# Reordered norm start and attention pair boundaries, and 64 moving columns in small matrix products of a hybrid diffusion backbone

## The chip, the cores and the metric

The kernel runs on one core of one Trainium2 chip. The metric is the device time of one execution in microseconds; of several executions the median is given. Everything below is on that single core: TensorE (PE in the profile, with its weight loads as PEld), VectorE (DVE), ScalarE (ACT), GpSimd (POOL) and SyncE (SP), which here only issues DMAs.

## The reference

A backbone of two layers over 512 latent and 256 context tokens of width 1024. Each layer normalises the tokens, shifts and scales them by vectors made from a condition, mixes them, and then runs a gated convolutional feed-forward network. Layer 0 mixes by retention with 4 heads, layer 1 by neighbourhood attention with 16 heads of width 64. Cut to what matters here:

```
for i in range(2):
    sh1, sc1, g1, sh2, sc2, g2 = split(silu(c) @ ada_w[i] + ada_b[i], 6)      # latent tokens
    csh1, csc1, ...            = split(silu(c_ctx) @ ada_w[i] + ada_b[i], 6)  # context tokens
    h  = rmsnorm(x, norm1_w[i]) * (1 + sc1) + sh1
    hc = rmsnorm(ctx, norm1_w[i]) * (1 + csc1) + csh1
    y, yc = retention(h, hc) if i == 0 else neighbourhood_attention(h, hc)
    x = x + g1 * y;  h2 = rmsnorm(x, norm2_w[i]) * (1 + sc2) + sh2;  x = x + g2 * conv_ffn(h2)
    # the same for ctx in layer 0
return rmsnorm(x, final_norm_w)
```

## The kernel before, in words

Activations lie with features on the 128 partitions: `x` is 8 blocks (k = 0 to 7) of 128 features by 768 tokens. Each large matrix is split into a high part and a rest (`w_hi`, `w_lo`, and `h_hi`, `h_lo`), and each product is three matrix products: high by high, high by rest, rest by high. `split()` on ACT makes `w_hi` from a raw 512 KB chunk (L873), `split()` on DVE makes `w_lo` (L1298), and `next_chunk()` on PE waits for it. SP streams the chunks through two slots. Each engine's order is written out by hand; semaphores join them.

**The start.** ACT squares the 8 blocks of `x`, DVE adds them, PE sums over partitions (`token_sums`, L448, with a moving operand `ones` of two columns), ACT takes roots (L903), DVE their reciprocals (`one_over`, L1329), and PE spreads them over the partitions (`spread_roots`, L455). ACT copies the spread row into `ss` (L930). Meanwhile SP has issued, in this order, `small`, `x`, the condition rows, and then for each k one 1 MB block `ada_start[k]`, with a raw weight chunk behind block 0 and block 2.

In `start_norm` DVE then goes through k = 0 to 7. `scale(k)` makes the scale vector by two multiply-and-reduce instructions over 1024 elements (L1340, L1342) and one small one (L1348). `shift(k)` takes the shift vector: for k in `PE_SHIFTS` = (1, 2, 4, 6, 7) PE makes it in `shift_row(k)` (L440: 8 matrix products, each recorded as two fp32 passes, with two moving columns) and DVE only adds a bias (L1357); for k = 0, 3, 5 DVE makes it with two more reductions and L1362. `rooted_x(k)` multiplies by the spread root (L1365), ACT applies scale and shift (L939) and rounds (`h_hi`, L943), and `low(k-1)` makes `h_lo` (L1369). For k = 2, 4, 6 a `split()` follows.

PE multiplies the normalised tokens with the first head's value weights (`token_values`, L538): for each k it waits for `h_lo` of that k and runs 18 products of 512 columns. `shift_row(4)`, `(6)` and `(7)` stand between them, and behind k = 4 also `idle(9)`, nine 128-column products whose result nobody reads (L465). Such fillers also stand ahead of it, in `start()`. After `token_values` PE runs the key and query projections (L403).

**The attention pairs.** In layer 1 two heads form a pair, c = 0 to 7. In `pair` PE runs `block_scores(i)` for 8 blocks (L689), `turn_probs(i)` (transposes of the probabilities, L697), the projections of the next pair in parts of a few products (`part`, L724: values, keys, queries), and `pair_values(0)`, `pair_values(1)` (L710). At a pair's end `turn_pair_values` transposes the next pair's values (L772). The next pair starts with `acc_taken[1]` and `q_taken`, then two block scores, then half of a value projection, then block score 2 and `turn_probs(0)`. `q_taken` counts once per pair, after both heads' queries have been split into `nq_hi` (four ACT instructions, L1193) and `nq_lo` (two DVE instructions, L1796).

After the queries ACT and DVE have a tail before the next pair's first maximum: a weight `split()`, `take_half(c, 1)` (L1209) and `add_halves(1)` (L1813), which finish the head output `both`; `take_turned_values` (L1201, L1806), which stores the transposed values and frees the accumulator that `turn_probs(0)` needs; and the split of `both` into `no_hi` and `no_lo` (L1235, L1846). Only then come `maximum(0)` (L1763), `exps(0)` (L1164), and `scale_probs(0)` (L1769, L1770), which `turn_probs(0)` waits for.

Of the kernel before, what the change touches and what calls it, by code (L numbers as in the profile page):

```python
# [37 lines left out]
P = 128  # L38
# [23 lines left out]
PE_SHIFTS = (1, 2, 4, 6, 7)  # L62
# [74 lines left out]
def backbone(nc, x_in, weights, ada_first, ada, cond_rows, small_in, bias_in, masks_in, park, out):  # L137
    ctx = ExitStack()
    with ctx:
# [88 lines left out]
        sums = o_ps[:, 3, 0:2 * TT]  # L228
        spread = o_ps[:, 0:2, :].rearrange("p a t -> p (a t)")
        shifts = [o_ps[:, n % 2, 2 * n:2 * n + 2] for n in range(len(PE_SHIFTS))]  # L230
# [136 lines left out]
        def _(pe):  # L367
# [43 lines left out]
            def start():  # L411

                pe.wait_ge(set_up, 1)
                idle(16, ones[:, :])
                pe.wait_ge(const_in, 16)
                for k in range(2, KC):
                    pe.wait_ge(sq_added, k)
                    idle(3)
                token_sums(KC, TOK)
                idle(4)  # L420
                pe.wait_ge(root_done, 1)
                idle(4)
                spread_roots(PARTS)
                idle(5)
                pe.wait_ge(cond_done, 1)
                shift_row(1)
                idle(4)
                shift_row(2)
                idle(12)

            def shift_row(k):

                n = PE_SHIFTS.index(k)
                pe.wait_ge(ada_start_in[k], 16)
                if n == 0:
                    pe.wait_ge(spread_copied, 1)
                elif n > 1:
                    pe.wait_ge(shift_taken, n - 1)
                for j in range(KC):
                    mm = nc.tensor.matmul(shifts[n], ada_start[k][:, 1, j * P:(j + 1) * P], silu_c[:, j, :],  # L440
                                          start=(j == 0), stop=(j == KC - 1))
                mm.then_inc(shift_made, 1)

            def token_sums(n, width):

                pe.wait_ge(sq_added, squares_added.up(n))
                for t in range(width // P):
                    mm = nc.tensor.matmul(sums[:, 2 * t:2 * t + 2], ss[:, t * P:(t + 1) * P], ones[:, 0:2], start=True, stop=True)  # L448
                mm.then_inc(sums_done, 1)
# [23 lines left out]
            def final_sums(width, ends=False):  # L473

                if not ends:
                    pe.wait_ge(lo_split, chunk.now() + 1)
                half = LAT if width == TOK else LAT // 2
                pe.wait_ge(sq_added, squares_added.up(KC) - 1)
                for t in range(width // P):
                    mm = nc.tensor.matmul(sums[:, 2 * t:2 * t + 2], ss[:, t * P:(t + 1) * P], ones[:, 0:2],  # L480
                                          start=(t == 0), stop=False)
                mm.then_inc(sq_added, 1)
                keep_busy(4)
                pe.wait_ge(sq_half, halves.up())
                for t in range(width // P):
                    if t == half // P:
                        pe.wait_ge(sq_done, squares_added.now())
                    mm = nc.tensor.matmul(sums[:, 2 * t:2 * t + 2], S[1][:, t * P:(t + 1) * P], ones[:, 0:2],
                                          start=False, stop=(t == width // P - 1))
                mm.then_inc(sums_done, 1)  # L490
# [32 lines left out]
            def token_values(first, ready):  # L523
# [3 lines left out]
                if first:  # L527
                    open_at(1)
                for s in range(4):
                    wh, wl = next_chunk()  # L530
                    for d in range(2):
                        k, last = 2 * s + d, s == 3 and d == 1
                        if ready is not None:
                            ready(k)
# [7 lines left out]
                        if first and k == 4:  # L542
                            idle(9, None, o_ps[:, 0, P:2 * P])
                            shift_row(PE_SHIFTS[4])
                    if s < 3:
                        mm.then_inc(v_used, 1)
                    if first and s < 2:
                        shift_row(PE_SHIFTS[2 + s])

# [183 lines left out]
            def queries():  # L733
                if q_left.began():
                    pe.wait_ge(q_taken, q_left.now())
                q_left.up()
# [38 lines left out]
            def pair(following):  # L775

                pe.wait_ge(acc_taken[1], A.taken[1].now())
                pe.wait_ge(q_taken, q_left.now())
# [7 lines left out]
                for i in range(8):  # L786
                    if i + 2 < 8:
                        block_scores(i + 2)
# [67 lines left out]
        def _(act):  # L856
# [41 lines left out]
            def root(n, width, loaded=False):  # L898
# [4 lines left out]
                nc.scalar.activation(rms[:, 0:t], sums[:, 0:2 * t].rearrange("p (t c) -> p t c", c=2)[:, :, 0],  # L903
# [306 lines left out]

            def pair(c, following):
# [32 lines left out]
            take_turned_values()  # L1244
# [31 lines left out]
        def _(dve):  # L1276
# [57 lines left out]
            def start_norm():  # L1334
# [3 lines left out]
                def row(k, r, made):  # L1338
# [6 lines left out]
                def scale(k):  # L1345
                    dve.wait_ge(ada_start_in[k], 16)
                    row(k, 0, k)
# [5 lines left out]
                def shift(k):  # L1353
                    if k in PE_SHIFTS:
                        n = PE_SHIFTS.index(k)
                        dve.wait_ge(shift_made, n + 1)
                        nc.vector.tensor_scalar(own_shift(k), shifts[n], ada_b[:, 0, k:k + 1], None, ALU.add)\  # L1357
# [8 lines left out]

                def low(k):
# [424 lines left out]
            def take_queries():  # L1792
# [5 lines left out]
                ins.then_inc(q_taken, 1)  # L1798
# [15 lines left out]

            def pair(c, following):
                dve.wait_ge(bias_done, biases_made.up(6))
                maximum(0)
                maximum(1)
                scale_probs(0)
                for i in range(8):  # L1820
# [4 lines left out]
                    probs_lo(i)  # L1825
                    if i == 5:
                        add_halves(0)
# [13 lines left out]
                add_halves(1)  # L1841
                if following:
                    take_turned_values()
# [14 lines left out]
            take_turned_values()  # L1858
# [191 lines left out]
```

## Time and profile before

| | |
|---|---|
| median of 3 executions | 2020.12 us (2018.02 to 2022.12) |
| the profiled execution, its own time | 2016.33 us |
| its span in the trace | 2014.4 us |
| PE busy | 1975.9 us, 98% of the span |
| DVE busy | 1293.6 us, 64% |
| ACT busy | 717.7 us, 36% |
| mean granted clock of PE | 0.994 of full speed |

The span is the stretch that the trace covers; 1.9 us of the execution lie around it. Busy time is that in which an engine has an instruction under way. The granted clock is the share of full speed (2.4 GHz) that PE was given: it is either 1.0 or 0.5 (1.2 GHz). The chain of waits is followed back from the last instruction, at each step to whatever released it.

### The profile page before, as it was taken

The numbers are of one execution on the slowest core, as the hardware profiler recorded it, in microseconds if no ns is written. First come the engines' busy times: TensorE is split into PE (matmuls) and PEld (weight loads), VectorE is DVE, ScalarE is ACT, GpSimd is POOL, SyncE is SP. The second block draws the span as 40 slices with busy tenths as digits, with TensorE's granted clock in tenths as the row PEclk, the third lists the DMA queues.
The fourth block names the chain that finished last, engine by engine and source line by source line (L and its number), as shares of the span: only waits on it lengthen the run. The fifth ranks groups of instructions, "written<-read, shape, count | busy, mean of one in ns | idle before, by whom it ended". The sixth has DMA issues, their size and how long they took to land.

```text
span 2014.4 us, 29078 instructions
## 1 busy us (share of the span) xinstructions
PE 1975.9 (98%) x10648; PEld 1692.1 (84%) x10648; DVE 1293.6 (64%) x1984; ACT 717.7 (36%) x1111; POOL 93.2 (5%) x161
## 2 busy tenths in 40 slices
PE   8999999999999999999999999999999999999998
PEld 7888888888888888888888888888888778788886
DVE  7866635744745677766664567766777677467376
ACT  5423223223313343312331233455555543234143
POOL 0000000000000000000000000111111000000000
PEclk8999999999999999999999999999999999999999
DMA  7231311221222112233224324421111322223223
GB/s 300 84 95 63 113 61 59 95 73 63 85 94 63 53 62 95 94 125 115 94 94 129 112 94 127 143 68 48 50 50 48 103 75 95 94 95 103 93 94 105
DMA packets 51268, 186.56 MB, mean 93 GB/s; under 512 B 5680, under 2 KB 5680, under 8 KB 51184
## 3 DMA queue, kind: packets, MB, share of 16 engines
q1 hardware_dynamic: 37744, 136.73, 20.6%
q0 software_dynamic: 13440, 48.63, 7.5%
q8 instruction: 62, 1.02, 0.2%
q14 instruction: 22, 0.18, 0.0%
HBM read 181.15 MB, written 4.19 MB: 92 GB/s over the span
## 4 chain that ended last, share of the span: by engine, by line
PE 90%; DVE 5%; ACT 2%; issue 1%; DMA 1%; SPq 0%; DVEq 0%; ACTq 0%; POOLq 0%
PE acc L403 60%; PE acc L724 5%; PE acc L664 4%; PE o_ps L538 4%; PE o_ps L574 3%; PE o_ps L724 2%; PE acc L538 2%; PE acc L561 2%; PE acc L503 2%; PE acc L759 2%; PE acc L697 1%; PE o_ps L689 1%; PE o_ps L710 1%; ACT nq_hi L1193 1%; DVE w_lo L1298 1%
## 5 line engine op out<-in xcount | busy, mean ns | idle before, releaser
L873 ACT ACTIVATE w_hi<-raw 128x1024 fp32r<-128x1024 f32 x223 | 235.7, 1057 | 582.7 <-PE acc L403 467.2
L1298 DVE TENSOR_TENSOR w_lo<-raw,w_hi 128x1024 fp32r<-128x1024 f32 x223 | 272.8, 1223 | 256.9 <-ACT w_hi L873 255.1
L403 PE MATMUL acc<-h_hi,w_hi 128*128 128x512 f32 x1520 | 434.4, 349 | 3.4 <-ACT u L1074 1.8
L403 PE MATMUL acc<-h_hi,w_lo 128*128 128x512 f32 x1520 | 434.8, 349 | 0.0
L403 PE MATMUL acc<-h_lo,w_hi 128*128 128x512 f32 x1520 | 434.7, 349 | 0.0
L403 PEld LDWEIGHTS acc<-h_hi,w_hi 128*128 128x128 f32 x1520 | 244.3, 188 | 43.9 <-ACT u L1074 2.5
L403 PEld LDWEIGHTS acc<-h_hi,w_lo 128*128 128x128 f32 x1520 | 244.4, 188 | 39.0
L403 PEld LDWEIGHTS acc<-h_lo,w_hi 128*128 128x128 f32 x1520 | 243.6, 188 | 38.4
L1467 DVE SCALAR_TENSOR_TENSOR x<-acc,mod,x 128x512 f32<-128x512 f32 (+3 forms) x137 | 82.0, 633 | 152.0 <-PE acc L403 121.8
L403 PE MATMUL acc<-act_hi,w_hi 128*128 128x512 f32 (+1 forms) x396 | 120.1, 357 | 2.0 <-DVE x L1467 2.0
L403 PE MATMUL acc<-act_hi,w_lo 128*128 128x512 f32 (+1 forms) x396 | 120.0, 357 | 0.0
L403 PE MATMUL acc<-act_lo,w_hi 128*128 128x512 f32 (+1 forms) x396 | 119.4, 355 | 0.0
L1409 DVE CUSTOM_DVE_ANT_0 ada_raw<-ada_raw,silu_rows 128x1024 f32<-128x1024 f32 x80 | 97.8, 1222 | 7.5 <-DMA ada_raw<-in_ada_dram 5.7
L320 POOL DMA_DIRECT2D ada_raw<-in_ada_dram x79 | 41.9, 530 | 1167.0 <-DVE mod_new L1409 1167.0
L1085 ACT ACTIVATE act_hi<-scratch 128x768 f32 (+3 forms) x44 | 32.6, 740 | 142.5 <-DVE scratch L1668 142.5
L1659 DVE SCALAR_TENSOR_TENSOR scratch<-u,taps,scratch 128x769 f32<-128x769 f32 (+1 forms) x88 | 78.0, 887 | 3.1
L1657 DVE SCALAR_TENSOR_TENSOR scratch<-u,taps,scratch 128x769 f32<-128x769 f32 (+1 forms) x88 | 78.0, 886 | 3.1
L403 PEld LDWEIGHTS acc<-act_hi,w_hi 128*128 128x128 f32 x396 | 65.0, 187 | 15.7 <-DVE x L1467 4.3
L403 PEld LDWEIGHTS acc<-act_lo,w_hi 128*128 128x128 f32 x396 | 65.1, 187 | 12.1
L403 PEld LDWEIGHTS acc<-act_hi,w_lo 128*128 128x128 f32 x396 | 65.1, 187 | 11.8
L1074 ACT ACTIVATE u<-acc 128x512 f32<-128x512 f32 (+1 forms) x132 | 63.0, 514 | 24.5 <-PE acc L403 24.5
L1172 ACT ACTIVATE pt_hi<-acc 128x512 fp32r<-128x512 f32 x64 | 38.5, 601 | 86.8 <-PE acc L697 86.7
(260 smaller groups left out, 3404.8 us busy)
## 6 DMA issues: line engine op xcount, KB each, us to landing
raw<-in_weights_dram SPq DMA_DIRECT2D x232, 512.0 KB, 3.4
ada_raw<-in_ada_dram POOLq DMA_DIRECT2D x80, 512.0 KB, 3.7
ada_start<-in_ada_first_dram SPq DMA_DIRECT2D x8, 1024.0 KB, 19.4
x<-in_x_in_dram SPq DMA_DIRECT2D x4, 768.0 KB, 7.0
park_dram<-x POOLq DMA_DIRECT2D x1, 2048.0 KB, 8.3
rel<-in_bias_dram POOLq DMA_DIRECT2D x16, 128.0 KB, 2.3
x<-park_dram POOLq DMA_DIRECT2D x2, 1024.0 KB, 6.6
out_dram<-x SPq DMA_DIRECT2D x8, 256.0 KB, 2.2
```

What stands on the lines that cost most here:

```text
L403: mm = nc.tensor.matmul(tile[:, c0:c0 + cn], wt[:, b * P:(b + 1) * P], mv[:, n, c0:c0 + cn], start=(n == 0 and m == 0), stop=(n == last an ...
L538: mm = nc.tensor.matmul(tile, hs[:, k, t * P:(t + 1) * P], ws[:, d * RV:(d + 1) * RV], start=(k == 0 and m == 0), stop=(last and m == 2))
L574: mm = nc.tensor.matmul(tile, vt[:, c0:c0 + P], pt[i % 2][:, p0:p0 + qn], start=((context or i == 0) and n == 0 and m == 0), stop=(i >= 5 ...
L664: mm = nc.tensor.matmul(tile[:, c0:c0 + cn], wt[:, n * P:(n + 1) * P], mv[:, n, c0:c0 + cn], start=(n == 0 and m == 0), stop=(n == size - ...
L724: mm = nc.tensor.matmul(tile[:, c0:c0 + cn], wt[:, n * P:(n + 1) * P], mv[:, n, c0:c0 + cn], start=(n == 0 and m == 0), stop=(n == KC - 1 ...
L873: nc.scalar.activation(w_hi[i][:, :] if spare is None else spare[0], raw[r][:, :], ACT.Copy).then_inc(hi_split, 1)
L1074: ins = nc.scalar.activation(u[j][:, c0 + c + 1:c0 + c + 1 + cn], tile[:, c0:c0 + cn], ACT.Copy)
L1298: nc.vector.tensor_tensor(lo, raw[r][:, :], hi.bitcast(F32), ALU.subtract).then_inc(lo_split, 1)
L1409: nc.vector.tensor_tensor_reduce(ada_raw[:, :], ada_raw[:, :], silu_rows[:, 0, :], 1.0, 0.0, ALU.mult, ALU.add, mod_new[:, j, 0:1]).then_i ...
L1467: ins = nc.vector.scalar_tensor_tensor(xv, tile[:, c0:c0 + cn], mod[:, layer, bass.ds(gate + m, 1), c:c + 1].rearrange("p a c -> p (a c)") ...
L1657: step(nc.vector.scalar_tensor_tensor(S[j][:, 0:width], u[j][:, 1:1 + width], tap(1), S[j][:, 0:width], ALU.mult, ALU.add))
L1659: nc.vector.scalar_tensor_tensor(S[j][:, 0:width], u[j][:, 2:2 + width], tap(2), S[j][:, 0:width], ALU.mult, ALU.add).then_inc(conv_done, 1)
```

## The change

It does four things. `PE_SHIFTS` becomes (0, 1, 2, 3, 5, 6, 7), so PE makes seven shift rows and DVE only that of k = 4; their places on PE move, and fillers and the wait for `root_done` are dropped or shortened. In `start_norm` ACT does its split and the `logs` instruction ahead of the copy of the spread row; DVE does `one_over` between the two reductions of `scale(0)`, and `rooted_x(0)` between those of `scale(1)`. Sums of squares and shift rows get 64 moving columns, copies of the old ones, wherever they stand in the program. In the attention pairs `q_taken` counts each head; the next pair starts after the first head's count; and `take_turned_values`, the second half, `no_hi` and `no_lo` move behind the first steps of the next pair.

```diff
-PE_SHIFTS = (1, 2, 4, 6, 7)
+WIDE = 64
+PE_SHIFTS = (0, 1, 2, 3, 5, 6, 7)
...
-        sums = o_ps[:, 3, 0:2 * TT]
+        sums = o_ps[:, 3, 0:WIDE * TT]
...
-        shifts = [o_ps[:, n % 2, 2 * n:2 * n + 2] for n in range(len(PE_SHIFTS))]
+        shifts = [acc[0][:, 0:WIDE]] + [o_ps[:, n % 2, WIDE * n:WIDE * (n + 1)] for n in range(1, len(PE_SHIFTS))]
...
                 token_sums(KC, TOK)
-                idle(4)
-                pe.wait_ge(root_done, 1)
-                idle(4)
+                pe.wait_ge(cond_done, 1)
+                shift_row(0)
                 spread_roots(PARTS)
-                idle(5)
-                pe.wait_ge(cond_done, 1)
+                idle(3)
                 shift_row(1)
-                idle(4)
+                idle(3)
                 shift_row(2)
-                idle(12)
+                idle(6)
...
-                if n == 0:
+                if n == 1:
                     pe.wait_ge(spread_copied, 1)
...
-                    mm = nc.tensor.matmul(shifts[n], ada_start[k][:, 1, j * P:(j + 1) * P], silu_c[:, j, :],
+                    mm = nc.tensor.matmul(shifts[n].rearrange("p (a c) -> p a c", c=2), ada_start[k][:, 1, j * P:(j + 1) * P],
+                                          silu_c[:, j:j + 1, :].to_broadcast([P, WIDE // 2, 2]),
                                           start=(j == 0), stop=(j == KC - 1))
...
-                    mm = nc.tensor.matmul(sums[:, 2 * t:2 * t + 2], ss[:, t * P:(t + 1) * P], ones[:, 0:2], start=True, stop=True)
+                    mm = nc.tensor.matmul(sums[:, WIDE * t:WIDE * (t + 1)], ss[:, t * P:(t + 1) * P], ones[:, 0:WIDE], start=True, stop=True)
...
                     open_at(1)
+                    pe.wait_ge(shift_taken, 1)
...
+                        if first and k and k + 2 in PE_SHIFTS:
+                            shift_row(k + 2)
                         if ready is not None:
                             ready(k)
...
-                        if first and k == 4:
-                            idle(9, None, o_ps[:, 0, P:2 * P])
-                            shift_row(PE_SHIFTS[4])
                     if s < 3:
                         mm.then_inc(v_used, 1)
-                    if first and s < 2:
-                        shift_row(PE_SHIFTS[2 + s])
...
-                q_left.up()
+                q_left.up(2)
...
-                pe.wait_ge(q_taken, q_left.now())
+                pe.wait_ge(q_taken, q_left.now() - 1)
                 block_scores(0)
                 block_scores(1)
...
                 for i in range(8):
+                    if i == 2:
+                        pe.wait_ge(q_taken, q_left.now())
...
+                split()
+                nc.scalar.activation(logs[:, :, 0:2], cols["dlog"].rearrange("p (h c) -> p h c", c=2), ACT.Exp)\
+                  .then_inc(logs_done, 1)
                 act.wait_ge(spread_done, 1)
                 nc.scalar.activation(ss[:, :], spread[:, 0:TOK], ACT.Copy).then_inc(spread_copied, 1)
-                nc.scalar.activation(logs[:, :, 0:2], cols["dlog"].rearrange("p (h c) -> p h c", c=2), ACT.Exp)\
-                  .then_inc(logs_done, 1)
-                split()
...
             def pair(c, following):
+                take_turned_values()
                 exps(0)
                 exps(1)
+                if c:
+                    take_half(c - 1, 1)
                 for i in range(8):
                     probs_hi(i)
                     if i + 2 < 8:
                         exps(i + 2)
+                    if c and i == 0:
+                        output_hi(c - 1)
...
-                take_half(c, 1)
-                if following:
-                    take_turned_values()
-                act.wait_ge(no_added, outs_added.up(2) + 1)
-                nc.scalar.activation(no_hi[:, bass.ds(c, 1), :].rearrange("p a t -> p (a t)"), both[:, :], ACT.Copy)\
-                  .then_inc(n_hi_done, 1)
+                else:
+                    take_half(c, 1)
+                    output_hi(c)
...
                     step(nc.vector.tensor_tensor_reduce(ada_raw[:, :], place, silu_rows[:, 1, :], 1.0, 0.0, ALU.mult,
                                                         ALU.add, mod_new[:, made, 1:2]))
+                    if between is not None:
+                        between()
...
-                scale(0)
-                one_over(TOK)
+                scale(0, lambda: one_over(TOK))
                 shift(0)
                 split()
-                dve.wait_ge(spread_copied, 1)
-                rooted_x(0)
                 for k in range(1, KC):
-                    scale(k)
+                    scale(k, first_rooted_x if k == 1 else None)
...
-                ins.then_inc(q_taken, 1)
+                    ins.then_inc(q_taken, 1)
...
                 maximum(0)
                 maximum(1)
+                take_turned_values()
                 scale_probs(0)
+                if c:
+                    add_halves(1)
                 for i in range(8):
...
                     probs_lo(i)
+                    if c and i == 0:
+                        output_lo(c - 1)
...
-                add_halves(1)
-                if following:
-                    take_turned_values()
-                dve.wait_ge(n_hi_done, n_hi_made.up(1))
-                hi, lo = (z[:, bass.ds(c, 1), :].rearrange("p a t -> p (a t)") for z in (no_hi, no_lo))
-                nc.vector.tensor_tensor(lo, both[:, :], hi.bitcast(F32), ALU.subtract).then_inc(no_lo_done, 1)
+                else:
+                    add_halves(1)
+                    output_lo(c)
```

`output_hi` and `output_lo` hold the instructions that make `no_hi` and `no_lo`, unchanged; `first_rooted_x` is the wait for `spread_copied` and `rooted_x(0)`. `final_sums` (L480, L488) gets the 64 columns in the same way, and the root on ACT reads every 64th column in place of every second.

## Rows read from the trace of the kernel before

**Rows 1.** The page: its head, and the chain that ended last, by engine
```profile
span 2014.4 us, 29078 instructions
...
PE 90%; DVE 5%; ACT 2%; issue 1%; DMA 1%; SPq 0%; DVEq 0%; ACTq 0%; POOLq 0%
```

**Rows 2.** Waits of PE, whole span: us in total, times, longest
```profile
PE o_ps L689 <- issue: 8.1, 8, 2.6
...
PE acc L697 <- DVE prob L1770: 1.6, 5, 0.8
```

**Rows 3.** Chain of waits, 58 to 80 us: start, us, engine and line
```profile
57.98 2.97 PE acc L538 x12
...
62.30 2.01 PE o_ps L465 x18
64.31 1.68 PE o_ps L440 x16
...
78.39 41.68 PE acc L403 x236
```

**Rows 4.** Chain of waits, 47 to 58 us, on DVE
```profile
47.72 0.12 DVE mod L1357
...
49.57 1.14 DVE w_lo L1298
50.70 1.14 DVE ada_raw L1340
...
53.15 0.29 DVE norm_a L1348
53.44 1.12 DVE ada_raw L1340
...
56.10 0.86 DVE scratch L1365
56.97 0.88 DVE h_lo L1369
```

**Rows 5.** DMA issues, us to landing: block 0 (at 4.29), block 1 (at 5.36), all
```profile
ada_start<-in_ada_first_dram SPq DMA_DIRECT2D x1, 1024.0 KB, 13.1
...
ada_start<-in_ada_first_dram SPq DMA_DIRECT2D x1, 1024.0 KB, 17.1
...
ada_start<-in_ada_first_dram SPq DMA_DIRECT2D x8, 1024.0 KB, 19.4
```

**Rows 6.** Timeline of ACT at 22 us: start, us, instruction, idle time before it
```profile
22.13 0.81 ACT L930 ACTIVATE ss<-o_ps 128x768 f32<-128x768 f32 x1 [3.81 <-PE o_ps L455]
```

**Rows 7.** Windows: length, busy of PE, PEld, DVE, ACT, POOL; clock; DMA
```profile
43.10:46.50 3.40, 1.89 (x11) 1.62 (x11) 3.37 (x6) 2.32 (x4) 0.00 (x0) 1.00 0.00 0
46.50:50.00 3.50, 3.50 (x11) 2.68 (x10) 3.46 (x7) 2.05 (x3) 0.00 (x0) 0.51 0.00 0
1312.50:1316.00 3.50, 0.85 (x9) 0.64 (x7) 1.38 (x2) 3.34 (x5) 2.74 (x6) 1.00 0.00 0
1316.40:1319.70 3.30, 3.30 (x14) 2.92 (x13) 3.11 (x7) 1.27 (x3) 0.00 (x1) 0.50 0.60 163
```

**Rows 8.** Timeline of a pair boundary, 1422 to 1431 us
```profile
1422.72 0.68 DVE L1796 SCALAR_TENSOR_TENSOR nq_lo<-o_ps,nq_hi 64x512 fp32r<-64x512 f32 x1 [1.08 <-ACT nq_hi L1193]
...
1424.68 0.33 PE L689 MATMUL o_ps<-nk,nq_hi 128*128 128x192 f32 x1 [0.77 <-issue]
...
1424.97 1.23 DVE L1298 TENSOR_TENSOR w_lo<-raw,w_hi 128x1024 fp32r<-128x1024 f32 x1 [0.39 <-ACT w_hi L873]
...
1426.95 1.02 DVE L1806 TENSOR_TENSOR nv<-acc,nv 128x384 fp32r<-128x384 f32 x2
...
1428.49 0.61 DVE L1763 CUSTOM_DVE_ANT_0 scratch<-o_ps,bias 128x448 f32<-128x448 f32 x1
...
1430.14 0.49 DVE L1770 TENSOR_SCALAR prob<-prob,top 128x512 f32<-128x512 f32 x1
...
1430.68 0.65 PE L697 MATMUL acc<-small,prob 128*128 128x128 f32 x4
```

More of the change, by code:

```diff
@@ L479, in final_sums @@
                 for t in range(width // P):
-                    mm = nc.tensor.matmul(sums[:, 2 * t:2 * t + 2], ss[:, t * P:(t + 1) * P], ones[:, 0:2],
+                    mm = nc.tensor.matmul(sums[:, WIDE * t:WIDE * (t + 1)], ss[:, t * P:(t + 1) * P], ones[:, 0:WIDE],
                                           start=(t == 0), stop=False)
@@ L487, in final_sums @@
                         pe.wait_ge(sq_done, squares_added.now())
-                    mm = nc.tensor.matmul(sums[:, 2 * t:2 * t + 2], S[1][:, t * P:(t + 1) * P], ones[:, 0:2],
+                    mm = nc.tensor.matmul(sums[:, WIDE * t:WIDE * (t + 1)], S[1][:, t * P:(t + 1) * P], ones[:, 0:WIDE],
                                           start=False, stop=(t == width // P - 1))
@@ L902, in root @@
                 t = width // P
-                nc.scalar.activation(rms[:, 0:t], sums[:, 0:2 * t].rearrange("p (t c) -> p t c", c=2)[:, :, 0],
+                nc.scalar.activation(rms[:, 0:t], sums[:, 0:WIDE * t].rearrange("p (t c) -> p t c", c=WIDE)[:, :, 0],
                                      ACT.Sqrt, bias=EPS, scale=1.0 / n).then_inc(root_done, 1)
@@ L1209, in take_half, with output_hi @@
                 nc.scalar.activation(both[hh * ND:(hh + 1) * ND, :], o_ps[0:ND, 0, :], ACT.Copy).then_inc(no_half, 1)
+            def output_hi(c):
+                act.wait_ge(no_added, outs_added.up(2) + 1)
+                nc.scalar.activation(no_hi[:, bass.ds(c, 1), :].rearrange("p a t -> p (a t)"), both[:, :], ACT.Copy)\
+                  .then_inc(n_hi_done, 1)
             def pair(c, following):
+                take_turned_values()
                 exps(0)
                 exps(1)
+                if c:
+                    take_half(c - 1, 1)
                 for i in range(8):
@@ L1336, in start_norm, with row @@
                 own_shift = lambda k: mod[:, 0, k, :]
-                def row(k, r, made):
+                def row(k, r, made, between=None):
                     place = ada_start[k][:, r, :]
@@ L1341, in row, with scale @@
                                                         ALU.add, mod_new[:, made, 1:2]))
+                    if between is not None:
+                        between()
                     step(nc.vector.tensor_tensor_reduce(place, place, silu_rows[:, 0, :], 1.0, 0.0, ALU.mult, ALU.add,
                                                         mod_new[:, made, 0:1]))
-                def scale(k):
+                def scale(k, between=None):
                     dve.wait_ge(ada_start_in[k], 16)
-                    row(k, 0, k)
+                    row(k, 0, k, between)
                     made = nc.vector.tensor_scalar(norm_a[:, k, :], mod_new[:, k, :], lift[:, k:k + 1], norm_w[:, 0, k:k + 1],
@@ L1356, in shift @@
                         dve.wait_ge(shift_made, n + 1)
-                        nc.vector.tensor_scalar(own_shift(k), shifts[n], ada_b[:, 0, k:k + 1], None, ALU.add)\
+                        nc.vector.tensor_scalar(own_shift(k), shifts[n][:, 0:2], ada_b[:, 0, k:k + 1], None, ALU.add)\
                           .then_inc(shift_taken, 1)
@@ L1365, in rooted_x, with first_rooted_x @@
                     nc.vector.tensor_tensor(S[2 + k % 2][:, 0:TOK], x[:, k, :], ss[:, :], ALU.mult).then_inc(norm_t, 1)
+                def first_rooted_x():
+                    dve.wait_ge(spread_copied, 1)
+                    rooted_x(0)
                 def low(k):
@@ L1813, in add_halves, with output_lo @@
                 nc.vector.tensor_tensor(own, own, o_ps[ND:P, 0, :], ALU.add).then_inc(no_added, 1)
+            def output_lo(c):
+                dve.wait_ge(n_hi_done, n_hi_made.up(1))
+                hi, lo = (z[:, bass.ds(c, 1), :].rearrange("p a t -> p (a t)") for z in (no_hi, no_lo))
+                nc.vector.tensor_tensor(lo, both[:, :], hi.bitcast(F32), ALU.subtract).then_inc(no_lo_done, 1)
             def pair(c, following):
@@ L1840, in pair @@
                     take_queries()
-                add_halves(1)
-                if following:
-                    take_turned_values()
-                dve.wait_ge(n_hi_done, n_hi_made.up(1))
-                hi, lo = (z[:, bass.ds(c, 1), :].rearrange("p a t -> p (a t)") for z in (no_hi, no_lo))
-                nc.vector.tensor_tensor(lo, both[:, :], hi.bitcast(F32), ALU.subtract).then_inc(no_lo_done, 1)
+                else:
+                    add_halves(1)
+                    output_lo(c)
             nc.vector.memset(top[:, 0, 5:6], 0.0).then_inc(s_taken, 1)
@@ L1857, in _ @@
             take_queries()
-            take_turned_values()
             pair(0, True)
```

## The prediction

> **What bounds the kernel now.** I read the page's head and its chain first: 90% of the chain is PE [rows 1], so the kernel can only get shorter where PE stands still, runs fillers on the path, or waits for another engine's chain. The waits of PE come next. The longest entry is the block scores at L689: 8.1 us in 8 times, the longest 2.6, so 5.5 us in the other seven, 0.79 each [rows 2]. Each stands at a pair boundary. "Issue" hides a semaphore; the timeline names it: the second `nq_lo` runs until about 1424.6 and PE starts at 1424.68 after 0.77 us idle, while the first head's was done at 1423.40 (1422.72 + 0.68) [rows 8]. The transposes L697 add 1.6 us of waiting for `scale_probs` [rows 2].
>
> The start does not show as a PE wait, because fillers fill it. The chain of waits shows it: until 57.84 it runs on DVE, from 57.98 on PE without a break, and the key projection starts at 78.39 [rows 3, 4]. What makes `token_values` end earlier is worth its full length, since PE alone is the path behind it.
>
> **The start, part by part.** From the DVE chain I take start-to-start times [rows 4]. Two reductions: 53.15 - 50.70 = 2.45. The small scale instruction: 0.29. A shift row made by PE: 0.12. One made by DVE: 56.10 - 53.44 = 2.66. `rooted_x` 0.86, `low` 0.88, `split` 1.13. So one k costs 4.60, with a DVE shift 7.14, with a split 1.13 more. Two rows (k = 0, 3, 5 before; k = 4 after) move to PE: 2 x 2.54 = 5.1 us less on DVE.
>
> Now the new schedule. `scale(0)` begins as before when block 0 has landed, at 4.29 + 13.1 = 17.4 [rows 5], and with the reciprocal inside takes to about 20.4; shift(0) needs PE's row: 16 passes at 0.105 (1.68 / 16) [rows 3] from 17.4 are done by 19.2. The split follows to 21.7. Then DVE must wait: block 1 lands only at 5.36 + 17.1 = 22.46 [rows 5]. The spread row is copied before that: before, the copy ended at 22.94 [rows 6], and its reciprocal came 1.3 us later than it will now. So `scale(1)` starts at 22.46 and, with `rooted_x(0)` inside, k = 1 ends at 22.46 + 4.60 + 0.9 = 28.0, which is `h_lo(0)`. Then: k = 2 gives `h_lo(1)` at 32.6, split 33.7; `h_lo(2)` 38.3; k = 4 with its DVE row gives `h_lo(3)` at 45.4, split 46.6; `h_lo(4)` 51.2; `h_lo(5)` 55.8, split 56.9; `h_lo(6)` 61.5. Later blocks are no limit: all eight are issued by 20 and land 19.4 us later [rows 5], at 39, and block 7 is wanted at 57.
>
> PE needs 18 products per k. From the end of the shift row (64.31 + 1.68 = 65.99) three k run to 78.39 [rows 3]: 12.4 / 3 = 4.1 each. Before, after the last stall: 4 k, the fillers 2.01 and a shift row 1.68 [rows 3], 57.98 + 16.4 + 3.7 = 78.1 against 78.39 read. After: k = 3 starts with `h_lo(3)` at 45.5; then 4.1 + 1.8 (row 6) + 4.1 + 1.8 (row 7) + 4.1 = 61.4, just when `h_lo(6)` comes at 61.5; two more k, 8.2, end at 69.8. Both chains agree, so neither has slack: **8.6 us** without any slow clock. I take **8.0**, since PE stands for 1.2 us before k = 3 beside a sparse shift row, and before the change such a place was followed by the half clock: PE busy 1.89 of 3.40 us at 43.1 to 46.5, then clock 0.51 [rows 7]. A stretch like that costs half of 3.4 = 1.7 us where PE is the path, and I count a third of one. The Trainium skill, page "TensorE: Matmul & The Clock Gate", section on the clock gate, speaks against the removed fillers: the throttled state is the default and activity is what releases it. By that rule alone the first product blocks would run at half clock too and the sum for the start would be nearer 6.
>
> What is moved on ACT: split and `logs` (with its table load) now run ahead of the spread copy. They fit between the root at 18.3 and the spread at about 21, and their price is zero; if they did not fit, the DVE wait for block 1 to 22.46 still covers 0.5 us. No DMA order changes. SP's reload behind the first split is asked for 5 us earlier, but it queues behind the blocks already issued.
>
> **64 columns.** No row shows 64 columns in fp32, so I bound it. Two columns: 0.105 us a pass; 128 columns: 2.01 / 18 = 0.112 [rows 3]. The 64 lie between, so 0.000 to 0.007 a pass. There are 112 shift passes and 140 in the sums (5 x 12 in `token_sums`, 80 in `final_sums`): 0 to 1.8 us, most of it in the start behind DVE. A gain is not excluded, as fuller passes may keep the full clock. I take 0, nearest to the middle of -2 (one low stretch less) and +1.8, and keep both ends.
>
> **The pair boundaries.** Removed: the wait for the second head, 0.77 us in pairs 1 to 7 and more in pair 0. PE starts its scores when the transposes end, at 1423.9. Then the question is what `turn_probs(0)` meets. Before, it started 6.00 us after the scores (1430.68 - 1424.68) [rows 8], and 0.2 to 0.3 of that was waiting for the probabilities. PE alone would be there at 1423.9 + 5.75 = 1429.7.
>
> The tail in new order on DVE: split to 1426.2 (unchanged, it waits for ACT) [rows 8]; `maximum(0)`, `(1)` at 0.61 and about 0.64 to 1427.5; turned values 0.93 (1.02 with its end) to 1428.4; `scale_probs(0)` 0.65 to 1429.1. `exps(0)` starts at 1426.9 and ends at 1427.7, before DVE wants it. The accumulator is free at 1428.4. So `turn_probs(0)` is free at 1429.1, 0.6 before PE comes: the wait is gone, and the pair is 0.77 + 0.2 = **0.97** shorter. The moved second half (0.69 on DVE), `no_hi` and `no_lo` (0.68 on DVE) now stand behind it: before `maximum(2)`, and before `maximum(3)`. What is queued behind them: `maximum(2)` ends at 1430.5 and `scale_probs(1)` at 1431.1, while PE wants probabilities 1 at 1432.9; a following pair's step is 3 us long on PE, so 1.4 us more of DVE work in two steps hides. If that cover were gone it would cost these 1.4 us. The wait for the second head, now before score 4, is over by 9 us.
>
> Pairs 1 to 6: 6 x 0.97 = 5.8. Pair 0: the stall of 2.6 [rows 2] shrinks to about 1.4, the first `nq_lo` instead of the second, and `turn_probs(0)` is held by its probabilities, which come 2.2 us earlier because two tail steps (0.93 on DVE and 1.0 of ACT's table load behind them) leave the path; and before, PE ran at clock 0.50 after that stall, having been busy 0.85 of 3.50 us [rows 7]. I take 2.0, between 1.2 and 2.2. Pair 7 has short PE steps (2.3 us), there DVE is nearly as busy, and the last half of pair 6 now falls into it; it gains 0.77 to 1.6, I take 0.9. Sum **8.7 us**.
>
> **Sum.** 8.0 + 8.7 + 0 = 16.7. The profiled execution took 2016.33 (span 2014.4 and 1.9 around it), so it would become 1999.6. That execution is 3.8 below the median of 2020.12; against the median the forecast is **2003.4**.
>
> **Rivals.** (A) *Slow clock in the catch-up.* Fewer fillers, and the first k runs at half clock, and pair 0 does so again. Price from rows: 1.7 us per low stretch [rows 7], two in the start, one in pair 0, of which 0.5 is in my sum already: 13 less instead of 16.7, rounded, 2007. For it: both low places before follow sparse PE work. Against: 64 columns are there in place of two. The page's rule named above would give this case. (B) *One of the two parts brings nothing*, because PE then waits for something just as long: for probabilities 0 at each boundary (my margin is 0.6 us), or in the start for DVE. 8.0 or 8.7 left: 2011.4 to 2012.1. Against: the margins above. (C) *The moved steps hold the first probabilities*, and the kernel is slower. Were the half, `no_hi`, and `no_lo` to stand before `turn_probs(0)` in effect, by an order between ACT and DVE that I misread, it would be free at 1429.1 + 2.6 = 1431.7, 1.0 later than before, and with the half clock after a 2 us stall (1.7 us, as after 1312.5 [rows 7]) each of 7 pairs loses 2.7: 2020.1 - 8.0 + 19 = 2031. It decides from 1431.8 on (8.0 / 7 = 1.1 later than before). Against it: `exps(0)` depends on none of them. (D) *The widened products are not free*: if each pass took 0.053 more, half of a 128-column pass on top, 252 x 0.053 = 13 us at most, 9 where PE is the path: 2012. Rows 3 speak against it, since 128 columns cost only 0.112.
>
> **How the numbers follow.** Forecast 0.64, A 0.20, B and D together 0.12, C 0.04. The range takes the forecast with its bounds (start 7 to 8.6, pair 0 and 7, columns -2 to +1.8, and half of the 4 us by which executions of one kernel differ) and A: 1999.0 to 2009.0; B, D and C, 0.16, lie outside. 0.2% is 4 us, about what a measurement of this kernel can tell from no change. Forecast, A and B all lie more than that below; some of B may measure within. Faster 0.93, same 0.04, slower 0.03.
>
> **What would show it.** In the profile after: the projection L403 starts near 70 instead of 78.39; the chain on DVE has only one pair of L1340/L1342 outside the scales, at k = 4; PE's wait at L689 falls from 8.1 to about 1.4 us; pairs repeat every 34.9 us instead of 35.9; the passes of L440 and L448 stay at 0.105 to 0.112 apart. I am wrong on the start if PE waits for `h_lo` at k = 6 or 7 beyond 62, or if a low clock stands between 46 and 62; wrong on the pairs if L697 waits more than 0.2 us a pair for L1770 or L1778.

## The result, and the profile after

The changed kernel takes 1995.92 us (median of 4, 1995.88 to 1996.99), the kernel before, timed beside it, 2020.88 (4 executions, 2018.02 to 2022.12). The ratio is 0.988 with a 95% interval of 0.9863 to 0.9897: 25 us, or 24 by the ratio, where 16.7 were forecast. The range ended at 1999.0, so the time lies 3.1 us below it. The profiled executions, 2016.33 and 1995.96, lie only 20.4 apart, since that of before lay 4.5 below the median of the executions timed here.

The page after, head and chain by engine, answering to [rows 1]:

```profile
span 1993.9 us, 29041 instructions
...
PE 94%; DVE 2%; ACT 1%; DMA 1%; issue 1%; SPq 0%; DVEq 0%; ACTq 0%; POOLq 0%
```

DVE fell from 5% of the chain to 2%: the start has moved over to PE. The waits of PE, answering to [rows 2] (us in total, times, longest):

```profile
PE o_ps L687 <- issue: 1.9, 1, 1.9
...
PE acc L695 <- DVE prob L1779: 0.9, 1, 0.9
```

L687 and L695 are L689 and L697 of before. The seven waits of 0.8 us at the block scores are gone; the 1.9 us left stand in pair 0, and the 0.9 us at L695 in pair 7. The chain in the start (start, us, engine and line), answering to [rows 3, 4]:

```profile
18.03 3.22 PE acc L439 x16
21.25 2.67 PE o_ps L455 x12
...
30.93 2.74 PE acc L541 x12
...
71.25 18.95 PE acc L404 x107
```

The key projection starts at 71.25 instead of 78.39, 7.1 us earlier. From 18.03 on, when block 0 has landed, the chain is PE alone, with 3.4 us of fillers in it, and PE never waits. The sixteen passes of shift row 0 took 3.22 us, 0.20 each, and not 0.105. The windows of the same execution (length, busy of PE, PEld, DVE, ACT, POOL, clock, DMA) show the half clock there. The timeline of DVE shows what that did to DVE, and how closely `h_lo(3)` came in time:

```profile
18.50:25.30 6.80, 6.80 (x34) 6.80 (x34) 5.29 (x11) 3.68 (x7) 0.00 (x0) 0.50 1.03 409
25.30:71.00 45.70, 45.70 (x258) 39.60 (x258) 40.65 (x67) 23.32 (x32) 0.69 (x1) 1.00 0.47 178
```
```profile
24.87 0.96 DVE L1373 TENSOR_TENSOR scratch<-x,ss 128x768 f32<-128x768 f32 x1 [1.08 <-ACT ss L933]
...
45.66 0.95 DVE L1381 TENSOR_TENSOR h_lo<-scratch,h_hi 128x768 fp32r<-128x768 f32 x1
...
55.97 0.95 DVE L1381 TENSOR_TENSOR h_lo<-scratch,h_hi 128x768 fp32r<-128x768 f32 x1
```

`h_lo(3)` ends at 46.6 and `h_lo(5)` at 56.9, 1.1 us behind my schedule. That is not the landing of block 0, which came 0.5 us later than before: `scale(1)` starts at 22.56, where 22.46 was forecast. It is the wait of 1.08 us for the copy of the spread row, which came late because shift row 0 and `spread_roots` ran at half clock. PE starts the products of k = 3 at 46.75, 0.1 behind `h_lo(3)`, so the two chains were all but tied. The pair boundary, answering to [rows 8]:

```profile
1409.30 0.68 DVE L1805 SCALAR_TENSOR_TENSOR nq_lo<-o_ps,nq_hi 64x512 fp32r<-64x512 f32 x1 [1.05 <-ACT nq_hi L1193]
...
1409.67 0.82 PE L770 MATMUL acc<-small,scratch 128*128 128x128 f32 x6
...
1410.24 0.34 PE L687 MATMUL o_ps<-nk,nq_hi 128*128 128x192 f32 x1
...
1413.97 1.02 DVE L1815 TENSOR_TENSOR nv<-acc,nv 128x384 fp32r<-128x384 f32 x2
...
1415.09 0.49 DVE L1779 TENSOR_SCALAR prob<-prob,top 128x512 f32<-128x512 f32 x1
...
1415.90 0.60 PE L695 MATMUL acc<-small,prob 128*128 128x128 f32 x4
```

The scores start 0.57 us after the transposes began; the first probabilities are ready at 1415.6, 0.3 before PE comes for them. A pair now takes 34.43 us instead of 35.88, from the start of the transposes of `turn_pair_values` to the next pair's, as the mean of pairs 1 to 6.

Where the 20.5 us of span lie, from the first start of a line in the two profiled executions:

| | before | after | gained in the stretch |
|---|---|---|---|
| key projection of head 0 starts | 78.2 | 71.1 | 7.1 |
| last retention output projection starts | 676.0 | 668.0 | 0.9 |
| pair 0, block scores start | 1315.8 | 1307.0 | 0.8 |
| attention's output products start (pair 7) | 1569.1 | 1549.0 | 11.3 |
| end of the span | 2014.4 | 1993.9 | 0.4 |

### The profile page after: what moved, and what is told of

Read it like the earlier page. It is cut to its first block, busy times and chain, and to the rows that moved or that the text cites. A ratio compares the mean times of both kernels' runs of the same rounds, so it can differ in the third digit from the quotient of the medians.

```text
span 1993.9 us, 29041 instructions
## 1 busy us (share of the span) xinstructions
PE 1964.6 (99%) x10628; PEld 1684.8 (84%) x10628; DVE 1288.7 (65%) x1976; ACT 717.5 (36%) x1111; POOL 93.0 (5%) x161
## 3 DMA queue, kind: packets, MB, share of 16 engines
q8 instruction: 62, 1.02, 0.2%
## 4 chain that ended last, share of the span: by engine, by line
PE 94%; DVE 2%; ACT 1%; DMA 1%; issue 1%; SPq 0%; DVEq 0%; ACTq 0%; POOLq 0%
PE acc L404 60%; PE acc L722 6%; PE o_ps L541 4%; PE acc L662 4%; PE o_ps L572 3%; PE acc L541 3%; PE o_ps L722 2%; PE acc L559 2%; PE acc L503 2%; PE acc L757 1%; PE o_ps L708 1%; PE o_ps L687 1%; PE acc L695 1%; DMA ada_start<-in_ada_first_dram 1%; PE o_ps L455 1%
## 5 line engine op out<-in xcount | busy, mean ns | idle before, releaser
L404 PE MATMUL acc<-h_hi,w_hi 128*128 128x512 f32 x1520 | 434.2, 349 | 3.5 <-ACT u L1074 1.8
L404 PE MATMUL acc<-h_lo,w_hi 128*128 128x512 f32 x1520 | 434.8, 349 | 0.0
L404 PE MATMUL acc<-h_hi,w_lo 128*128 128x512 f32 x1520 | 433.7, 348 | 0.0
L404 PEld LDWEIGHTS acc<-h_hi,w_hi 128*128 128x128 f32 x1520 | 243.6, 188 | 43.4 <-ACT u L1074 2.6
L404 PEld LDWEIGHTS acc<-h_hi,w_lo 128*128 128x128 f32 x1520 | 244.5, 188 | 39.3
L404 PEld LDWEIGHTS acc<-h_lo,w_hi 128*128 128x128 f32 x1520 | 243.6, 188 | 38.2
L404 PE MATMUL acc<-act_hi,w_hi 128*128 128x512 f32 (+1 forms) x396 | 119.9, 356 | 1.3 <-DVE x L1476 1.3
L404 PE MATMUL acc<-act_hi,w_lo 128*128 128x512 f32 (+1 forms) x396 | 120.2, 357 | 0.0
L404 PE MATMUL acc<-act_lo,w_hi 128*128 128x512 f32 (+1 forms) x396 | 119.5, 355 | 0.0
L404 PEld LDWEIGHTS acc<-act_hi,w_hi 128*128 128x128 f32 x396 | 65.1, 187 | 15.1 <-DVE x L1476 3.5
L404 PEld LDWEIGHTS acc<-act_lo,w_hi 128*128 128x128 f32 x396 | 65.1, 188 | 12.1
L404 PEld LDWEIGHTS acc<-act_hi,w_lo 128*128 128x128 f32 x396 | 65.1, 187 | 11.6
```

Source lines behind the costliest of these rows:

```text
L404: mm = nc.tensor.matmul(tile[:, c0:c0 + cn], wt[:, b * P:(b + 1) * P], mv[:, n, c0:c0 + cn], start=(n == 0 and m == 0), stop=(n == last an ...
```

## The experiments

Ratios are to the kernel before, run in turn with each kernel on the same chip. Over these jobs its medians were 2019.36 to 2020.01, with executions from 2015.22 to 2022.69.

**Start alone (start2).** The hunks in `start`, `shift_row`, `token_values` and `start_norm`, with two columns, pairs as before:

```diff
-WIDE = 64
+WIDE = 2
```

> Only the start is reordered (shift rows, fillers, order on ACT and DVE), moving operands keep two columns, the pairs stay as before. If the parts are independent, the median falls by about 7 us against the kernel before, as the projection moved from 78.39 to 71.25 in the changed kernel's profile. If the start with two columns runs into more half-clock stretches than with 64, it falls by 4 to 6 only.

2010.94 (2010.58 to 2013.06), ratio 0.9963 (0.9951 to 0.9976): 7.5 us by the ratio, 9.1 by the medians, so the first expectation by its number. The sign named for the second was there too: in its profile the projection starts at 74.32, 3 us later than in the changed kernel, with the clock at 0.90 from 10 to 80 us.

**Pair boundaries alone (attn).** Only the hunks of the two `q_taken` waits, `pair`, `output_hi` and `output_lo`.

> Only the pair boundaries are reordered. Theory 1: the profile of the changed kernel shows a pair period of 34.43 in place of 35.88 us, so six pairs give 8.7, pair 0 about 2.5 and pair 7 under 1: 11 to 12 us less than before, all of it here. Theory 2: my forecast's 0.97 a pair and 8.7 in all, the rest being an effect of the widened products.

2007.57 (2002.6 to 2010.04), ratio 0.9937 (0.9924 to 0.9951): 12.4 us by medians, 12.7 by the ratio. Theory 1, by a little more than it said. The scores of pair 0 and the output products of pair 7 start 242.4 us apart (before: 253.3; changed kernel: 242.0), so the columns have no part in this.

**64 columns alone (wide).** The kernel before with

```diff
+WIDE = 64
 PE_SHIFTS = (1, 2, 4, 6, 7)
...
-idle(9, None, o_ps[:, 0, P:2 * P])
+idle(9, None, o_ps[:, 0, 3 * P:4 * P])
```

and the changed `sums`, `shifts`, products and root.

> Only the 64 moving columns, in the shift rows and the sums of the kernel before (one filler writes another part of its bank). Theory 1: executions of the kernel before differ by 4 us because sparse stretches of PE sometimes bring the half clock; 64 columns make those stretches fuller, so the median falls by 3 to 5 us and the executions come within 1.5 us of each other. Theory 2: the columns do nothing, 0 within 1 us and the same spread as before. Theory 3, my forecast's bound: up to 1.8 us slower.

2015.30 (2013.03 to 2017.84), ratio 0.998 (0.9971 to 0.9989): 4.0 to 4.7 us faster, as theory 1 said, neither nothing nor slower. The executions still spread over almost 5 us (7.5 in the kernel before beside it), so that part of theory 1 failed. A row of windows of the kernel before shows pair 0 at the low level [rows 7]; from 1270 to 1330 us its mean clock was 0.94, here 1.00.

**All but the columns (both2).** The changed kernel with `WIDE = 2`.

> The whole change, but with two moving columns. Theory 1: 19 to 21 us less than before, 4 to 5 above the changed kernel, with executions that differ by 4 us. Theory 2: the changed kernel's 25 us less, since the columns do nothing. Its clock shows half-clock stretches where the changed kernel had none if theory 1 holds.

2000.53 (2000.03 to 2002.89), ratio 0.991 (0.9897 to 0.9922). Theory 1: 19.5 us, and the last 4.6 are the columns'. Its chain in the start:

```profile
17.45 3.54 PE acc L439 x16
...
33.42 3.15 PE acc L541 x12
...
73.81 16.24 PE acc L404 x92
```

PE's first product starts 2.5 us later than with 64 columns and everything behind it is later by the same, 73.81 against 71.25. Its executions spread by 2.9 us only, not by the 4 expected. The intervals of both2 and of the changed kernel touch (at 0.9897 in the first job, 0.99 in the later one), but the executions lie apart: 2000.03 is the lowest here, 1997.26 the highest of the changed kernel's eight.

**The early start of the pair alone (qsplit).** The kernel before with only

```diff
-                pe.wait_ge(q_taken, q_left.now())
+                pe.wait_ge(q_taken, q_left.now() - 1)
...
-                ins.then_inc(q_taken, 1)
+                    ins.then_inc(q_taken, 1)
```

`q_left.up(2)` to match, and the second wait ahead of score 4.

> The kernel before, with q_taken counted per head and PE starting the next pair after the first head; the tail of ACT and DVE keeps its old place. Theory 1: the first transposes L697 depend on probabilities that come no earlier than before (1430.6 in the pair read), so PE gives nearly all of it back there: 0 to 2 us less in all, with L697 waiting about 1 us a pair. Theory 2: the wait removed at L689 is worth itself, 0.8 to 1.1 us a pair, 7 us or more.

2019.15 (2017.4 to 2022.74), ratio 0.9999 (0.999 to 1.0008): nothing. Theory 1. The wait moved down one step (waits of PE):

```profile
PE acc L697 <- DVE prob L1772: 6.8, 8, 1.4
...
PE o_ps L689 <- DVE top L1765: 2.5, 7, 1.5
```

**The moved tail alone (tail).** `take_turned_values`, `take_half(c, 1)`, `add_halves(1)`, `output_hi` and `output_lo` moved, PE still waiting for both heads.

> The kernel before, with only the tail moved behind the first steps of the next pair; PE still waits for both heads' queries. Theory 1: PE's stall at L689 stays (0.77 us idle, but 1.1 from start to start), only the wait at L697 goes, 0.28 us a pair and about 1 us in pair 0: 2 to 4 us less. The two halves together gave 12, so they need each other. Theory 2: the halves add, 12 less what the wait alone gives.

2016.44 (2013.34 to 2019.73), ratio 0.9982 (0.9973 to 0.9991), 3.3 us. Theory 1. The other wait stands as in [rows 2]:

```profile
PE o_ps L689 <- issue: 8.1, 8, 2.6
```

With qsplit and tail the sum is 0.6 + 3.3 = 3.9; together (attn) they give 12.4.

**Fillers ahead of shift row 0 (warm).**

```diff
                 token_sums(KC, TOK)
+                idle(6)
                 pe.wait_ge(cond_done, 1)
```

> The changed kernel with six 128-column fillers between the sums of squares and shift row 0, where PE was idle and sparse before the half-clock stretch of 18.5 to 25.3 us. Theory 1: that stretch delays PE's first product to 30.9 us and PE never waits after it, so if the fillers keep the full clock, the first product starts at about 29 and DVE becomes the bound: the projection starts 0.6 to 1.5 us earlier than 71.25. Rival: the half clock there comes from elsewhere and stays, then 0 to 0.5 us slower.

1995.72 (1994.43 to 1996.65), ratio 0.9883 (0.9868 to 0.9898). In its profile PE kept the full clock, DVE's chain bounds until `h_lo(3)`, and the projection starts at 69.08:

```profile
43.62 0.88 DVE h_lo L1382
44.54 3.01 PE acc L542 x12
...
69.08 21.07 PE acc L404 x119
```

But the time is that of the changed kernel beside it, and the 0.6 to 1.5 us of theory 1 do not show in the median.

**The changed kernel again (after2).**

> The changed kernel again, unedited, on the chip of the runs beside it. All theories: 1996 us within 1.5, and executions within 1.5 us of each other, while those of the kernel before differ by 4 or more.

1995.84 (1994.23 to 1997.26), ratio 0.9884 (0.9869 to 0.99). This profiled execution (span 1992.8), the same program as above, had no low clock in the start. PE's shift row 2 waits for block 2, which lands at 25.55, and six fillers stand between it and the first products:

```profile
5.88 19.67 DMA ada_start<-in_ada_first_dram
25.59 2.00 PE o_ps L439 x16
...
28.99 2.76 PE acc L541 x12
...
69.39 20.71 PE acc L404 x117
```

The projection at 69.39 is close to the 69.8 that the forecast's schedule gave at the full clock. In shift64, warm and warm2, also at full clock there, the chain is the forecast's own: DVE up to `h_lo(3)`, PE from k = 3 at 44.5 to 45.2 (forecast 45.5), the projection at 69.67, 69.08 and 69.82. The two executions of one program did nearly the same before they parted: from 12 to 18 us, at full clock in both, PE was busy 4.79 of 6.00 us in the first and 4.65 here. So the stretch at half clock in the first profile is a matter of the execution, and what warm does to it can't be told from chance with one profile each; its median says that it does not pay.

**Which columns (sum64, shift64).** The changed kernel with 64 columns only in the sums of squares (sum64, first two lines, and the products to match), or only in the shift rows (shift64, the other two).

```diff
-shifts = [acc[0][:, 0:WIDE]] + [o_ps[:, n % 2, WIDE * n:WIDE * (n + 1)] for n in range(1, len(PE_SHIFTS))]
+shifts = [acc[0][:, 0:2]] + [o_ps[:, n % 2, WIDE * n:WIDE * n + 2] for n in range(1, len(PE_SHIFTS))]
...
-sums = o_ps[:, 3, 0:WIDE * TT]
+sums = o_ps[:, 3, 0:2 * TT]
```

> The changed kernel with two columns in the shift rows and 64 only in the sums of squares. The whole change with two columns everywhere took 2000.5, with 64 everywhere 1995.9. Theory 1: most of the 4.6 us lies in the start, where the shift rows are the sparse work: 1999 to 2001, half clock again before 36 us, none at 710, 1280 and 1311. Theory 2: it lies at the three sums ahead of the norms and at pair 0: 1996 to 1997.

> The changed kernel with 64 columns only in the shift rows and two in the sums of squares. Theory 1: 1996 to 1998, the start as in the changed kernel, at most one low stretch near 1280 or 1311. Theory 2: 1999 to 2001.

sum64: 1998.13 (1996.93 to 1999.54), ratio 0.9892 (0.9875 to 0.9908). shift64: 1997.30 (1996.61 to 1998.72), ratio 0.9889 (0.9872 to 0.9905). By the times neither theory: shift64 is within theory 1, sum64 is 0.9 below it; each half brings some of the 4.6 us, and the intervals overlap. The profiles show what theory 1 named. With two-column shift rows the start is at 0.90 from 10 to 80 us and the projection at 73.68; with two-column sums the start is at 1.00 and it stands at 69.67, but a low stretch of 3.4 us lies at 1307, in pair 0. That stretch alone says nothing of the sums, since warm2 below has it with 64 columns. Taken together the profiles say more: between 700 and 1600 us each of the seven kernels with two-column sums has one to three low stretches, some right behind the sums (in the kernel before the sums run from 1276.8 and the clock is low from 1282.2), and the seven profiles with 64-column sums have one in all.

**Shift row 3 back on DVE (dve3).**

```diff
-PE_SHIFTS = (0, 1, 2, 3, 5, 6, 7)
+PE_SHIFTS = (0, 1, 2, 5, 6, 7)
```

> The changed kernel with the shift row of k = 3 given back to DVE (two reductions, 2.54 us more on DVE, 1.73 less on PE). My theory: DVE's chain and PE's chain tie within 0.5 us in the start, so the whole 2.5 us comes back: 2.0 to 2.6 us slower than the changed kernel, and PE waits for h_lo. Rival: PE's late first product is the bound with slack on DVE, then 0.5 slower to 1.5 faster.

1996.90 (1996.64 to 2000.1), ratio 0.989 (0.9873 to 0.9906): 1.0 above the changed kernel, between my theory and the rival. In its profile the projection starts at 71.87, 2.5 later than in after2, but not all of that is DVE's row: PE's clock was low from 40.2 to 43.6, and the first twelve products of k = 2 took 4.57 us, where 3.0 is the time at full clock. Without that it would be about 70.3 (an estimate), 0.9 later than after2. PE waits once for `h_lo`, 3.5 us, and then has one row less to make, which is the part of the 2.5 us that comes back:

```profile
PE acc L541 <- DVE h_lo L1381: 3.5, 1, 3.5
```

**Fillers everywhere in the start (warm2).** As warm, and

```diff
-                idle(3)
+                idle(7)
                 shift_row(1)
-                idle(3)
+                idle(4)
                 shift_row(2)
-                idle(6)
+                idle(4)
```

> The changed kernel with six fillers ahead of shift row 0, seven and four in place of three and three ahead of shift rows 1 and 2, four in place of six behind row 2, so that PE is not idle while it waits for the spread row and for block 2. Theory 1: what is left between executions of the changed kernel (1994.2 to 1997.3) is half clock in the start; every execution then lies near the best, 1994 to 1995.5, with the projection starting at 69. Rival: the spread comes from elsewhere, and nothing changes in median or spread, 1996 within 1.

1996.01 (1994.33 to 1997.34), ratio 0.988 (0.9864 to 0.9897). The rival: same median, same spread. The start was at full clock from 15 on and the projection at 69.82, yet the span was 1995.4; a low stretch lay at 1307 to 1310, in pair 0. None of the versions beats the changed kernel by more than its executions differ.

The mean granted clock of PE in two stretches, one profile each, for eleven of the profiles (dve3, warm and warm2 are 0.98 to 1.00 in the first stretch), with the first start of L403 or L404, 0.1 to 0.2 ahead of the chain's:

| kernel | columns | 10 to 80 us | 1270 to 1330 us | projection starts |
|---|---|---|---|---|
| before | 2 | 0.93 | 0.94 | 78.2 |
| attn, start code of before | 2 | 0.93 | 0.97 | 80.9 |
| qsplit, start code of before | 2 | 0.90 | 0.97 | 80.5 |
| tail, start code of before | 2 | 0.88 | 1.00 | 81.6 |
| wide, old start | 64 | 0.95 | 1.00 | 79.8 |
| start2 | 2 | 0.90 | 0.94 | 74.2 |
| both2 | 2 | 0.90 | 0.94 | 73.7 |
| sum64 | 2 in the shifts | 0.90 | 1.00 | 73.5 |
| shift64 | 2 in the sums | 1.00 | 0.97 | 69.5 |
| changed | 64 | 0.95 | 1.00 | 71.1 |
| changed, again | 64 | 1.00 | 1.00 | 69.2 |

## Why the prediction was right and wrong

**The bound** was read rightly: PE's chain, broken at the pair boundaries and preceded by DVE's in the start. Both reordered parts gained, and the sign held. The forecast fell short by 8.3 us (25.0 measured, 16.7 forecast). The steps that failed are two terms of the sum. One is the 0.97 us of a pair, which measured 1.45, or 2.9 us over six pairs. The other is the columns, taken at 0, which measured 4.6. The start's 8.0 held alone (7.5 to 9.1). Without the columns the whole change gave 19.5 us (both2), 2.8 more than the sum; the remaining 0.9 is the difference between the two medians of the kernel before, 2020.88 and 2020.01. Of the signs of being wrong that the prediction named none appeared (L695 waits once, 0.9 us in pair 7): they all looked for a smaller gain, none for a larger one.

**The start** was forecast at 8.0 and measured 7.1 between the two profiled executions. DVE's schedule held to 1.1 us, and at full clock the end came at 69.1 to 69.8 as worked out (after2, shift64, warm, warm2). A step that failed here is the price of "16 passes at 0.105": at half clock they took 0.20, the spread row was copied after `scale(1)` had begun and not before, and the first product started at 30.9. I had looked for the low level in the catch-up at 43 to 46 and counted a third of 1.7 us; in the first profile it came before the first product. Rival A named "the first k runs at half clock", and its place was off by one stage only. With 64 columns the first products themselves ran at full clock. "Later blocks are no limit" did not hold either, since shift row 2 waited for block 2 in after2, but PE made that up by k = 3.

**The baseline** makes the closeness of 7.1 to 8.0 partly luck, for both ends were off. The sum was worked from one execution, 2016.33, and carried to a median 3.8 higher as if the 3.8 were alike in both kernels. Four other kernels with the old start (attn, qsplit, tail and wide) reached the projection at 80.0 to 81.8 in the chain, not at 78.39. In each of them the first twelve products behind DVE's chain took 4.4 to 4.6 us where the profile before has 2.97 [rows 3]: a low stretch that it was spared. With the new start and two columns in the rows the projection stands at 73.7 to 74.3 (start2, both2, sum64), about 7 us earlier. With 64 columns and a full clock it stands at 69.1 to 69.8, 4 us earlier again, and that belongs to the columns. These are one profile each.

**64 columns**: "I take 0" was the failed step. Their cost was right, 16 passes in 1.73 us against 1.68, 0.003 a pass. Their gain was bounded by one low stretch, 2 us; it measured 4.0 to 4.7 (wide) and 4.6 (both2 against the changed kernel). The trace of before had four low stretches ahead of the span's end, at 46.5 and in pair 0 [rows 7] and these two:

```profile
26.20:33.00 6.80, 6.80 (x33) 6.80 (x33) 6.73 (x11) 3.83 (x6) 0.00 (x0) 0.50 1.02 409
...
1282.00:1286.00 4.00, 4.00 (x17) 3.49 (x16) 3.06 (x5) 1.34 (x3) 1.32 (x3) 0.57 0.15 36
```

But the chain runs on DVE at 26, at 46 and from 1282.9 on, so only the stretch in pair 0 delayed PE by its whole cost, and that trace alone could not have given 4.6. What it hid is that other executions have such stretches on PE's path. In the new start the gain lies before the first product, as above. Where the 4 us of wide lie is not shown: its profile has no low stretch in pair 0, but one at 57.6 to 61.0, on the path. Rival D (widened products not free) is refuted.

**The pair boundaries**: 8.7 forecast. From the transposes ahead of pair 0 on, the two profiles give 11.8, of which the table above has 11.3, as it begins at pair 0's scores; attn measured 12.4. The mechanism was right to the step: qsplit alone gives 0, tail alone 3.3, both 12.4, as PE's next wait, for the probabilities, ends at the same time as before unless the tail moves too. The mis-sized term is "0.77 + 0.2 = 0.97" a pair, measured 35.88 - 34.43 = 1.45. The 0.77 is the idle time that the profile writes, counted from the modelled end of the transposes. From start to start they and the scores were 1.59 apart (the transposes began at 1423.09, the scores at 1424.68 [rows 8]) and are now 0.57: 1.02. The step from score 2 to the transposes shrank from 0.76 to 0.48, and the projection ahead of it by 0.07: 0.35 where I had 0.2. The last 0.08 I have not traced. Six pairs by 0.48 are 2.9, nearly the whole miss here. Pair 7 gained 1.0 at its boundary (0.9 forecast) and gave 0.3 of it back inside, where its chain now runs through the moved tail on ACT and DVE (`no_hi`, `no_lo` of pair 6, which PE wants at i = 1). Pair 0 kept 1.9 of its 2.6 us wait, not 1.4, but gained the half clock that followed: 2.35 us in all, where I had 2.0.

**Rivals.** A did not hold as a whole; B and C are excluded by the alone-runs. Start2, attn and wide add up to 9.1 + 12.4 + 4.7 = 26.2 by medians against 24 to 25 together: they are nearly independent.

**Open**: which of the two kinds of columns is worth more (0.8 us between their medians, inside the intervals), and whether the low stretch in pair 0 accounts for all of the 3 us by which executions of the changed kernel still differ. Why two columns and 64 leave different clocks behind is not shown, only that they did.

## What to carry to other kernels

Price a PE stall from start to start against the same step without a stall; the idle column counts from the modelled end of the product before and here gave 0.77 of 1.02 us. A wait is worth something only up to the next wait behind it: look for the pair of edits that belong together, for each alone gave 0 and 3 us of 12. And where executions differ by more than the terms of the sum, one profile is one draw: look for what varies (here the granted clock in sparse stretches of PE) and count it as a term. Filling up such a stretch was nearly free here, 0.003 us a pass for 64 columns in place of two.

## What was unexpected in the hardware

A matrix product with 2 moving columns and one with 64 take nearly the same time, 0.105 and 0.108 us a pass, but the clock afterwards was not the same. In all seven kernels with two columns in the shift rows, sum64 included, the mean clock from 10 to 80 us was 0.88 to 0.93; in the seven profiles with 64 it was 0.95 to 1.00. PE was "busy" by the profile in both. That is one profile of each kernel and two of the changed one. The level is also not fixed by the program: one program had 6.8 us at 1.2 GHz in the start in one execution and none in the next. And six or nine more fillers, with which PE was busy 64.2 of the 65 us from 15 on, moved the median by 0.2 us at most and left the executions 2.2 and 3.0 us apart (3.0 without them).
